# One of a block pair's two pre-made weight sums: made in its on-chip buffer by a load and an adding transfer instead of ahead in DRAM

## What is computed

```python
def swiglu_block(x, w_gate, w_up, w_down, scale):
    h = rms_norm(x, g)
    return x + scale * ((silu(h @ w_gate) * (h @ w_up)) @ w_down)
```

## Time and profile before

| what | us |
|---|---|
| median of 3 runs | 1271.07 (1268.37 to 1271.60) |
| the profiled execution's own time | 1270.26 |
| its span | 1268.5 |
| TensorE matmuls busy | 1256.2 (99%) |
| VectorE busy | 991.6 (78%) |
| ScalarE busy | 843.3 (66%) |
| GpSimd busy | 68.4 (5%) |
| DMA moved | 331.90 MB, 262 GB/s on the mean |

### The profile page before, as it was taken

How to read it: one execution, slowest core, us unless ns; L and a number is a source line. 1 busy time by engine, 2 the same in 40 slices (tenths; PEclk the granted TensorE clock), 3 DMA queues, 4 the chain that set the end, 5 groups by cost and what they waited for, 6 DMA issues and landing times.

```text
span 1268.5 us, 17171 instructions
## 1 busy us (share of the span) xinstructions
PE 1256.2 (99%) x6858; PEld 1051.5 (83%) x6858; DVE 991.6 (78%) x1151; ACT 843.3 (66%) x1083; POOL 68.4 (5%) x100
## 2 busy tenths in 40 slices
PE   9999999999999999999999999999999999999998
PEld 7888888889988888887788887888888898888887
DVE  5888777877657888786488778678887798688885
ACT  7576658766556666586466667666665857766763
POOL 0000000000000000000000001000000100000000
PEclk9999999999999999999999999999999999999999
DMA  9997748887696799868688886768898988857772
GB/s 342 319 320 233 247 162 283 265 266 217 186 301 264 254 303 313 304 220 257 231 298 298 233 261 196 274 253 249 316 296 288 311 266 270 309 206 267 272 242 76
DMA packets 49279, 331.90 MB, mean 262 GB/s; under 512 B 5484, under 2 KB 7788, under 8 KB 10160
## 3 DMA queue, kind: packets, MB, share of 16 engines
q1 hardware_dynamic: 34512, 230.88, 47.4%
q0 software_dynamic: 13536, 97.27, 31.1%
q10 hardware_dynamic: 1152, 2.66, 0.6%
HBM read 329.73 MB, written 65.02 MB: 311 GB/s over the span
## 4 chain that ended last, share of the span: by engine, by line
PE 97%; DVE 2%; DMA 1%; ACT 0%; issue 0%; SPq 0%; DVEq 0%; ACTq 0%
PE ps L2903 25%; PE ps L2905 25%; PE ps L2904 25%; PE ps L2813 8%; PE ps L3036 2%; PE ps L2924 1%; PE ps L2932 1%; PE ps L2937 1%; PE ps L580 1%; PE ps L2829 1%; PE ps L582 1%; PE ps L581 1%; PE ps L2947 1%; DVE w_lo_part L1755 1%; PE ps L2876 1%; DMA w_raw<-in_tiles 1%
## 5 line engine op out<-in xcount | busy, mean ns | idle before, releaser
L1755 DVE TENSOR_TENSOR w_lo_part<-w_raw,w_hi_part 128x2048 fp32r<-128x2048 f32 (+2 forms) x181 | 409.2, 2265 | 58.5 <-ACT w_hi_part L712 57.9
L712 ACT ACTIVATE w_hi_part<-w_raw 128x2048 fp32r<-128x2048 f32 (+1 forms) x180 | 341.3, 1898 | 99.0 <-PE ps L2905 80.8
L2903 PE MATMUL ps<-w_hi_part,x_hi 128*128 128x512 f32 (+1 forms) x680 | 266.7, 392 | 1.3 <-ACT mem_kv L1259 0.8
L2905 PE MATMUL ps<-w_hi_part,x_lo 128*128 128x512 f32 (+1 forms) x680 | 258.8, 381 | 0.0
L2904 PE MATMUL ps<-w_lo_part,x_hi 128*128 128x512 f32 (+1 forms) x680 | 258.2, 380 | 0.0
L1755 DVE TENSOR_TENSOR w_lo_part<-arena,w_hi_part 128x2048 fp32r<-128x2048 f32 x78 | 178.4, 2288 | 38.2 <-ACT w_hi_part L712 38.2
L712 ACT ACTIVATE w_hi_part<-arena 128x2048 fp32r<-128x2048 f32 x78 | 149.4, 1915 | 71.7 <-PE ps L2905 66.0
L2903 PE MATMUL ps<-w_hi_part,h_hi_part 128*128 128x512 f32 x464 | 183.8, 396 | 0.0
L2905 PE MATMUL ps<-w_hi_part,h_lo_part 128*128 128x512 f32 x464 | 180.9, 390 | 0.0
L2904 PE MATMUL ps<-w_lo_part,h_hi_part 128*128 128x512 f32 x464 | 180.8, 390 | 0.0
L2903 PEld LDWEIGHTS ps<-w_hi_part,x_hi 128*128 128x128 f32 x680 | 128.0, 188 | 25.3 <-issue 1.4
(11 more groups left out here) (457 smaller groups left out, 1601.8 us busy)
## 6 DMA issues: line engine op xcount, KB each, us to landing
w_raw<-in_tiles SPq DMA_DIRECT2D x176, 1024.0 KB, 6.9
made_sums<-in_tiles POOLq DMA_DIRECT2D x60, 1024.0 KB, 8.2
arena<-made_sums SPq DMA_DIRECT2D x30, 1024.0 KB, 8.2
arena<-in_tiles POOLq DMA_DIRECT2D x21, 1024.0 KB, 10.7
arena<-in_tiles SPq DMA_DIRECT2D x9, 1024.0 KB, 8.1
mem_kv<-in_tiles POOLq DMA_DIRECT2D x6, 1024.0 KB, 10.9
w_raw<-in_tiles SPq DMA_DIRECT2D x3, 512.0 KB, 6.5
arena<-in_w_ukv POOLq DMA_DIRECT2D x1, 1536.0 KB, 6.8
```

Source lines behind the costliest of these rows:

```text
L712: nc.scalar.activation(WH[:, n % RING, 0:w], source(n), ACT.Copy).then_inc(S["w_hi"], 1)
L1755: nc.vector.tensor_tensor(WL[:, n % RING, 0:w], source(n), WH[:, n % RING, 0:w], ALU.subtract).then_inc(S["w_split"], 1)
L2903: nc.tensor.matmul(o, a_hi, w_hi, start=start, stop=False, skip_group_check=True)
L2905: return nc.tensor.matmul(o, a_lo, w_hi, start=False, stop=stop, skip_group_check=True)
```

## The change

T1 is still made in DRAM and loaded. T3 is no longer made there: SP loads the plain tile g0(s+1) into TC, and GpSimd, when that has landed, adds g1(s+1) into TC by an adding transfer (`t3_sum`). ScalarE waits for the new semaphore `t3_sum`. `made_sums` has half the size, and GpSimd's list has 15 copies and 15 adds into DRAM less and 15 adding transfers into TC more; the sums that stay are made at other places of the list. SP's first T1 and T3 loads of ffn1, ffn3 and ffn4 and the second T1 load stand further back in its order. ffn2's keep their places. The line of semaphore names, where `t3_sum` is added, is left out here.

```diff
--- before.py
+++ after.py
@@ -286,7 +286,7 @@
     ROW = MH * 2 * SEQ
     bias_line = nc.dram_tensor("bias_line", [ROW], f32, kind="Internal")
     bias_rows = nc.dram_tensor("bias_rows", [P * (ROW + 1)], f32, kind="Internal")
-    made = nc.dram_tensor("made_sums", [sum(len(steps_of(name)) for name in QUADS), 2, P, TILE], f32, kind="Internal")
+    made = nc.dram_tensor("made_sums", [sum(len(steps_of(name)) for name in QUADS), P, TILE], f32, kind="Internal")
 
     with ExitStack() as ctx:
         enter = ctx.enter_context
@@ -543,8 +543,11 @@
         def t3_loaded(name, s):
             return S["q_loaded2"], 16 * (n_pairs + quad_no(name, s) + 1)
 
-        def made_sum(name, s, k):
-            return S["base_loaded"], 16 * (2 * n_pairs + 4 * quad_no(name, s) + 2 * k + 2)
+        def t3_added(name, s):
+            return S["t3_sum"], 16 * (quad_no(name, s) + 1)
+
+        def made_sum(name, s):
+            return S["base_loaded"], 16 * (2 * n_pairs + 2 * quad_no(name, s) + 2)
 
         def t4_added(name, s):
             return S["t_added"], 16 * (2 * n_pairs + quad_no(name, s) + 1)
@@ -617,9 +620,12 @@
 
             def t_load(name, s, k):
 
-                dst, (sem, _) = ((ta_of(name, s), t1_loaded(name, s)), (TC, t3_loaded(name, s)))[k]
-                sp.wait_ge(*made_sum(name, s, k))
-                sp.dma_start(dst, made[quad_no(name, s), k, :, :]).then_inc(sem, 16)
+                if k == 0:
+                    sp.wait_ge(*made_sum(name, s))
+                    sp.dma_start(ta_of(name, s), made[quad_no(name, s), :, :]).then_inc(t1_loaded(name, s)[0], 16)
+                else:
+                    t = stored0[name] + stored_at("g0", s + 1)
+                    sp.dma_start(TC, d["tiles"][t, :, :]).then_inc(t3_loaded(name, s)[0], 16)
 
             def later_loads(kind, name, s):
 
@@ -649,14 +655,14 @@
                     t_load("ffn2", 5, 1)
                     t_load("ffn2", 7, 0)
                 for name in QUADS:
-                    if name != "ffn2" and n == unit_of[name, "g1", 1]:
-                        sp.wait_ge(S["x_ready"], 4 * (X_OF[name] - 1) + 1)
+                    if name != "ffn2" and n == unit_of[name, "g0", 2]:
+                        sp.wait_ge(S["norm_sd"], norm_no[name] + 1)
                         t_load(name, 3, 0)
-                    if name != "ffn2" and n == unit_of[name, "d", 0]:
-                        sp.wait_ge(S["norm_sd"], norm_no[name] + 1)
+                    if name != "ffn2" and n == unit_of[name, "m2", 3]:
                         if name == "ffn3":
                             sp.wait_ge(S["bias_dma"], 16)
                         t_load(name, 3, 1)
+                    if name != "ffn2" and n == unit_of[name, "m1", 3]:
                         t_load(name, 5, 0)
                     for s in steps_of(name)[1:]:
                         if n == unit_of[name, "m1", s]:
@@ -716,7 +722,7 @@
                 if name in QUADS and kind == "m6":
                     act.wait_ge(S["sums"], sum_no[name, "t2", s])
                 elif name in QUADS:
-                    act.wait_ge(*{"p5": t1_loaded, "m7": t3_loaded, "m4": t4_added}[kind](name, s))
+                    act.wait_ge(*{"p5": t1_loaded, "m7": t3_added, "m4": t4_added}[kind](name, s))
                 elif kind in ("p5", "m7"):
                     act.wait_ge(S["t_added"], 32 * pair_no(name, s) + (16 if kind == "p5" else 32))
                 elif kind in ("m6", "m4"):
@@ -4130,18 +4136,18 @@
                 return d["tiles"][stored0[name] + stored_at(kind, s), :, :]
 
             def made_block(name, i):
-                return made[quad_no(name, steps_of(name)[i // 2]), i % 2, :, :]
+                return made[quad_no(name, steps_of(name)[i]), :, :]
 
             def copy(name, i):
 
-                pool.wait_ge(S["base_loaded"], 16 * (2 * n_pairs + 4 * quad_no(name, steps_of(name)[0]) + 2 * i))
-                pool.dma_start(made_block(name, i), stored(name, "g0", steps_of(name)[i // 2] + i % 2),
+                pool.wait_ge(S["base_loaded"], 16 * (2 * n_pairs + 2 * quad_no(name, steps_of(name)[i])))
+                pool.dma_start(made_block(name, i), stored(name, "g0", steps_of(name)[i]),
                                max_dma_last_dim=4 * TILE).then_inc(S["base_loaded"], 16)
 
             def add(name, i):
 
-                pool.wait_ge(S["base_loaded"], 16 * (2 * n_pairs + 4 * quad_no(name, steps_of(name)[0]) + 2 * i + 1))
-                pool.dma_start(made_block(name, i), stored(name, ("g0", "g1")[i % 2], steps_of(name)[i // 2] + 1), accum_op=ALU.add,
+                pool.wait_ge(S["base_loaded"], 16 * (2 * n_pairs + 2 * quad_no(name, steps_of(name)[i]) + 1))
+                pool.dma_start(made_block(name, i), stored(name, "g0", steps_of(name)[i] + 1), accum_op=ALU.add,
                                max_dma_last_dim=4 * TILE).then_inc(S["base_loaded"], 16)
 
             def paced(n):
@@ -4156,8 +4162,14 @@
                     if n != units[-1]:
                         copy(name, i + 1)
 
+            def t3_sum(name, s):
+
+                pool.wait_ge(*t3_loaded(name, s))
+                pool.dma_start(TC, stored(name, "g1", s + 1), accum_op=ALU.add).then_inc(t3_added(name, s)[0], 16)
+
             def t4_sum(name, s):
 
+                t3_sum(name, s)
                 split(name, "m6", s)
                 pool.dma_start(ta_of(name, s), stored(name, "g1", s), accum_op=ALU.add).then_inc(t4_added(name, s)[0], 16)
 
@@ -4169,59 +4181,33 @@
             for s in PAIR_STEPS:
                 pair_sums("ffn0", s)
             paced(tile0["ain"])
-            makes("ffn1", 0, [tile0["ain"] + 2 * t + 1 for t in range(6)] + [tile0["mem"], tile0["mem"] + 1])
+            makes("ffn1", 0, [tile0["ain"] + 2 * t + 1 for t in range(4)])
+            makes("ffn2", 0, [tile0["ain"] + 9, tile0["ain"] + 11, tile0["mem"]])
+            makes("ffn3", 0, [tile0["mem"] + 1])
             paced(tile0["mem"] + 2)
-            makes("ffn2", 0, [tile0["mem"] + 3])
-            make("ffn2", 1)
-            make("ffn2", 2)
-            t4_sum("ffn1", 3)
-            split("ffn1", "m4", 3)
-            copy("ffn2", 3)
-            t4_sum("ffn1", 5)
-            split("ffn1", "m4", 5)
-            add("ffn2", 3)
-            t4_sum("ffn1", 7)
-            split("ffn1", "m4", 7)
-            copy("ffn2", 4)
-            t4_sum("ffn1", 9)
+            makes("ffn3", 1, [tile0["mem"] + 3])
+            for s in steps_of("ffn1"):
+                t4_sum("ffn1", s)
             pool.wait_ge(S["tile_used"], unit_of["ffn1", "m7", 9] + 1)
             pool.dma_start(KVD, d["w_dkv"].rearrange("p (a b) -> p a b", b=2 * P + ROPE)).then_inc(S["side_loaded"], 16)
             split("ffn1", "m4", 9)
             pool.dma_start(KVU, d["w_ukv"].rearrange("p (a b) -> p a b", b=2 * BH * P)).then_inc(S["side_loaded"], 16)
-            split("ffn2", "g0", 1)
-            add("ffn2", 4)
             split("ffn2", "d", 0)
-            makes("ffn2", 5, [unit_of["ffn2", "g0", 2]])
-            makes("ffn3", 0, [unit_of["ffn2", "d", 1], unit_of["ffn2", "d", 2]])
-            t4_sum("ffn2", 5)
-            split("ffn2", "m4", 5)
-            copy("ffn3", 2)
-            t4_sum("ffn2", 7)
-            split("ffn2", "m4", 7)
-            add("ffn3", 2)
-            t4_sum("ffn2", 9)
+            makes("ffn3", 2, [unit_of["ffn2", "d", 1]])
+            for s in steps_of("ffn2"):
+                t4_sum("ffn2", s)
             split("ffn2", "m4", 9)
             pool.dma_start(RELB[:, :], d["rel_bias"]).then_inc(S["side_loaded"], 16)
             pool.dma_start(TABLE, d["rel_table"]).then_inc(S["side_loaded"], 16)
-            makes("ffn3", 3, [tile0["bin"], tile0["bin"] + 1, tile0["uq"] + 1])
+            makes("ffn3", 3, [tile0["bin"]])
+            makes("ffn4", 0, [tile0["bin"] + 1, tile0["uq"] + 1])
             pool.wait_ge(S["bias_row"], 1)
 
             pool.dma_start(bass.AP(bias_line, 0, [[2 * SEQ, MH], [1, 2 * SEQ]]), BROW).then_inc(S["bias_dma"], 16)
             pool.wait_ge(S["bias_dma"], 16)
-            makes("ffn3", 6, [tile0["out1"]])
-            paced(tile0["out1"] + 1)
-            copy("ffn3", 7)
-            t4_sum("ffn3", 3)
-            split("ffn3", "m4", 3)
-            add("ffn3", 7)
-            t4_sum("ffn3", 5)
-            split("ffn3", "m4", 5)
-            copy("ffn4", 0)
-            t4_sum("ffn3", 7)
-            split("ffn3", "m4", 7)
-            add("ffn4", 0)
-            t4_sum("ffn3", 9)
-            make("ffn4", 1)
+            makes("ffn4", 2, [tile0["out1"]])
+            for s in steps_of("ffn3"):
+                t4_sum("ffn3", s)
             pool.dma_start(bass.AP(bias_rows, 0, [[ROW + 1, P], [1, ROW]]),
                            bass.AP(bias_line, 0, [[0, P], [1, ROW]])).then_inc(S["bias_dma"], 16)
             pool.wait_ge(S["bias_dma"], 32)
@@ -4231,9 +4217,7 @@
 
                 src = bass.AP(bias_rows, SEQ - 1 - tb * P, [[ROW, P], [2 * SEQ, MH], [1, (tb + 1) * P]])
```

(6 more changed lines are left out.)

## The result

| | before | changed |
|---|---|---|
| median of 4 runs, us | 1270.29 (1268.37 to 1271.60) | 1287.29 (1283.68 to 1291.61) |
| the profiled execution's own time, us | 1270.26 | 1283.68 |
| its span, us | 1268.5 | 1281.9 |

The changed kernel takes 1.0129 times as long (95% interval 1.0111 to 1.0147). That is slower by far more than 0.3%, and outside the range of the prediction (1268.0 to 1274.8). The forecast "within 0.3%" was wrong.

The account below looks back on a forecast made before the run. The prediction took TensorE to bound the kernel, busy 1256.2 of 1268.5 us. From the profiled 1270.26, plus 2.0 at m7(5) of ffn2, minus 1.55 ahead of in2, it forecast 1270.7 us, range 1268.0 to 1274.8.

Parts of the forecast that it names:

- within 0.3%: Whole kernel: time stays the same, 1267.3 to 1274.9 us around 1271.07; chance 0.85.
- First pairs of ffn1, ffn3, ffn4 ... Cost 0: First pairs of three blocks: T3's chain of 19 to 25 us fits its 29 us; cost 0.
- The T1 loads that are moved back have similar room: First pairs of ffn1, ffn3, ffn4: T1 loads moved back also land in time; cost 0.
- Part 1: Whole kernel: 30 transfers into DRAM go, 15 adding transfers into TC come; the saved traffic is priced at 0.
- rival 3: In ffn2, slower: adds into TC run against each other and the ring; 1276.0 us with A = 16; chance 0.11.
- Part 2, pair 5 of ffn2: At m7(5) of ffn2 T3 comes late and TensorE waits A - 8.7, 2.0 us at the median A.
- Part 2, steady pairs at 0: Pairs 5, 7 and 9 at their steady place: T3 ready after 18.9 us, 3.6 us in time; cost 0.
- signs of being wrong: TensorE waiting at m7 of pair 7 or 9, pairs not 30.89 us long, or T3 adds landing above 13 us.
- Part 3: End of ffn3: bias_rows issued earlier lets the ring load land before in2, removing TensorE's wait; gain 1.55 us.
- A: Landing time of a T3 add, taken from the T4 adds: 8.5 to 12.9 us, median 10.7.

Follow-up runs that it names:

- add_held: The changed kernel with the T3 add of pair 3 in ffn1, ffn3 and ffn4 held until m2(3) is split; 1277.17 us, ratio 1.0043.
- t1_back: The changed kernel with only the T1 load of pair 5 in ffn1, ffn3 and ffn4 moved behind the ring load of p3(3); 1276.99 us, ratio 1.0044.
- early: The changed kernel with SP's first T1 and T3 loads of ffn1, ffn3, ffn4 and pair 5's T1 put back to old places; 1276.34 us, ratio 1.0045.
- the repetition: The changed kernel run again unaltered, also called changed again, against the kernel before; 1286.46 us, ratio 1.0112.
- no_add: The changed kernel without the 15 T3 adds, T3 taken as the plain tile g0(s+1); 1268.83 us, ratio 0.9983.
- tables_first: The kernel before with the second sum of ffn4 made behind the mixer's tables, not ahead of them; 1275.16 us, ratio 1.0026.
- one_onchip: The kernel before with only T3 of ffn4's pair 3 made in TC by a load and an adding transfer; 1269.47 us, ratio 0.999.
- both: The two repairs in the changed kernel: first T1 and T3 loads at old places, T3 of ffn2's pair 5 made in DRAM; 1271.36 us, ratio 1.0004.

## Why the prediction was wrong, step by step

- **"First pairs of ffn1, ffn3, ffn4 ... Cost 0" is the step that failed.** It compared T3's own chain of 19 to 25 us with its room of 29, and that was right: T3 is in time there in every trace. It didn't ask what the new add, issued at 398.92, does to the ring load issued 0.3 us later, while the moved T1 load is also still in flight. In place of 0 the three blocks cost 2.61 + 2.38 + 2.02 = 7.0 us of waits in the profiled execution, 7.9 us by the start times, and 9.3 to 10.1 us by the medians of `add_held`, `t1_back` and `early` against the repetition of the changed kernel. "The T1 loads that are moved back have similar room" was true of T1 as well, and beside the point in the same way.
- **Part 1, added transfers at 0 by the pair windows, was drawn from the wrong rows.** The earlier trace rows show that TensorE is no slower at a DMA share of 0.94 than of 0.77. They say nothing of how long one ring load takes among neighbours, and that decides whether the window is kept. The row that could have warned was the earlier trace rows, a ring load of 11.3 us. The prediction put it down to `bias_rows` alone, but by the earlier trace rows the add issued at 972.01 was in flight beside it too (it landed at 980.6). The prediction used that row for in2 and, in rival 3, for ffn2 only.
- **Part 2, pair 5 of ffn2, was right in place, cause and size**: add 10.8 us against 10.7, wait 2.42 against 2.0. Of the 0.4 us more, 0.3 pass between the load's landing (646.8) and the add's issue (647.13), which the sum had as one moment. Missing was what the wait costs behind it, about 2 us of granted clock, so the place costs 4.3 us by the start times (4.6 by the windows) where the sum had 2.0.
- **Part 2, steady pairs at 0, was wrong by 2.9 us.** T3 itself is in time in all of them, and where no load is late they take 30.89 us. The 15 adds land after 8.2 to 13.3 us, median 9.1. But in four of them a ring load issued 1 to 3 us behind the add is late: in ffn4 the one issued at 1234.18, 1.3 us behind the add, lands after 9.2 us, ScalarE waits 2.41 us for it and TensorE 0.94. It is the same mistake as in the first pairs. Of the prediction's signs of being wrong, longer pairs came, and so did landings above 13 us (13.3 in ffn1, 13.2 in ffn3). No m7 of a pair 7 or 9 waited.
- **Part 3 was right.** The wait of 1.55 us is gone in the changed kernel, `no_add`, `tables_first` and `one_onchip`, and TensorE gains 1.8 us there by the start times. `bias_rows` takes 15.8 us and the ring load 8.1, both about 1 us more than forecast, and the ring load has that room.
- **Rival 3** had the right sign, and its words "adds into TC run against each other and against the ring" are half of the mechanism. But its place was ffn2 and its price a later T3, which didn't come (A stayed at 10.8, below its 14.9). The ring load was the one to be late, in three other blocks, and so the range ended 9 us under the fastest of the four runs.

**The sum again.** In the profiled executions the spans differ by 13.4 us. By the start times they are 7.9 for the three m1(3), which the prediction had at 0, 4.3 for m7(5), which it had at 2.0, 2.9 for the steady pairs, which it had at 0, and -1.8 for in2, which it had at -1.55. By the medians the two repairs together give back 15.1 of 15.5 us.

**What stays open.** The medians put both repairs higher than the profiled executions do (10.1 and 7.3 us against 7.9 and 4.3). In the repetition TensorE loses some 1.5 us more in ffn3, where its clock fell once more (see below), so other executions may well lose more than the first profiled one. That wasn't shown for those that weren't profiled.

## What to carry to other kernels

When a transfer is added or moved, don't only ask whether its own data is in time: list every transfer in flight beside it, and hold each one's landing, lengthened by what its neighbours cost, against its own room. The one with the least room pays, and here that was the plain load of the ring and not the moved sum. A new transfer that must start at such a place is cheap once it or one neighbour is moved: here a move of 5 to 16 us was worth 9 to 10 us by the medians, in each of three edits.

## What the runs showed of the hardware

- A ring load of 1 MB, p3(3), lands after 4.6 to 4.9 us with nothing new beside it (once 5.7, in ffn3 of `both`), after 6.7 to 9.0 with two other transfers of 1 MB ahead of it, and after 12.8 to 13.4 with three (12.3 to 13.1 in the repetition). Block by block the first two neighbours together add 2 to 4 us, and the third adds 4 to 6, whether the one left out is the add or T1's load.
- A wait of 2.4 us can cost nearly as much again in granted clock, but not always. At m7(5) of ffn2 the clock fell in four traces, behind waits of 2.28 to 3.21 us (`add_held`, changed, changed again, `t1_back`), and stayed at 1.00 in the fifth, `early`, behind 2.58 us. In the changed kernel it stayed at 1.00 behind 2.61 us at 417.29 and 2.38 at 868.89. In the repetition it fell at the latter place, behind 2.33 us:

```profile
868.55:872.00 3.45, 3.45 (x11) 2.80 (x12) 3.45 (x2) 0.66 (x2) 0.00 (x0) 0.72 0.65 221
...
872.00:876.00 4.00, 4.00 (x16) 3.14 (x16) 2.75 (x3) 1.91 (x1) 0.86 (x1) 0.81 1.08 358
```

So the length of one wait doesn't settle whether the clock falls. The clock explains little of the 8 us over which the changed kernel's first four runs spread: their mean granted clocks are 0.998, 0.997, 0.996 and 0.997 from the fastest to the slowest, a thousandth of the time is 1.3 us, and the second and the slowest lie 6.7 us apart at the same 0.997. What spreads them stays open. The runs of `no_add`, which has no such waits, lie within 2 us.
